# A transformer and two mixer layers in one kernel: the first modulated norm by quarters instead of halves, with the other modulation pieces loaded behind each round's weights

## The reference

```python
mod = silu(c) @ w_ada + b_ada                 # c: 1 x 1024, w_ada: 1024 x 6144
sh1, sc1, g1, sh2, sc2, g2 = split(mod, 6)
h = rms_norm(x, norm1_g) * (1 + sc1) + sh1    # 256 x 1024
proj = h @ w_in                               # 1024 x 12800: rq, rk, rv, rg, 9 attention tiles, 2 gates
...                                           # retention: rotary, scores, group norm per head, gate
x = x + g1 * token_mixer(h)
h = rms_norm(x, norm2_g) * (1 + sc2) + sh2    # and so on
```

## Time and profile before

| what | us |
| --- | --- |
| median of 3 runs (1368.62 to 1371.56) | 1368.72 |
| the profiled execution | 1369.16 |
| its span, first to last instruction | 1367.4 |
| TensorE busy | 1309.5 |
| VectorE busy | 881.9 |
| ScalarE busy | 736.4 |
| GpSimd busy | 638.9 |

### The profile page before, as it was taken

The page is one execution under the profiler, slowest core; times in us unless marked ns, Lnnn a source line. Parts: engine busy times, 40 slices in busy tenths (PEclk is TensorE's granted clock), DMA queues, the critical chain, the costliest instruction groups (busy, mean ns, idle before and its releaser), DMA issues.

```text
span 1367.4 us, 18658 instructions
## 1 busy us (share of the span) xinstructions
PE 1309.5 (96%) x6684; PEld 1085.4 (79%) x6684; DVE 881.9 (64%) x1383; ACT 736.4 (54%) x1107; POOL 638.9 (47%) x512
## 2 busy tenths in 40 slices
PE   7999999999998999999999999999989999899997
PEld 4778787899886788888787787888868877788885
DVE  6684873345343565223678667888868867788777
ACT  5343444444464544445566428666745663567664
POOL 3898888988858699999400420000051034000000
...
GB/s 375 312 262 305 157 243 292 242 182 245 187 154 142 167 185 188 197 191 183 203 127 81 1 21 315 313 289 336 281 186 182 94 31 1 222 316 293 283 312 97
DMA packets 45496, 280.03 MB, mean 205 GB/s; under 512 B 5565, under 2 KB 8893, under 8 KB 13918
## 3 DMA queue, kind: packets, MB, share of 16 engines
...
## 4 chain that ended last, share of the span: by engine, by line
PE 74%; DVE 11%; POOL 5%; DVEq 3%; ACT 3%; issue 2%; DMA 1%; ACTq 1%; SPq 0%; POOLq 0%
PE AC L1302 9%; PE AC L1304 9%; PE AC L1303 9%; PE G L1302 8%; PE G L1304 8%; PE G L1303 8%; POOL w_lo L721 5%; PE T L1492 2%; PE G L1492 2%; DVE w_lo L2172 2%; DMA w_raw<-w_stream 1%; PE G L1340 1%; PE G L1339 1%; PE G L1338 1%; PE T L1493 1%
## 5 line engine op out<-in xcount | busy, mean ns | idle before, releaser
L721 POOL TENSOR_TENSOR w_lo<-w_raw,w_hi 128x512 fp32r<-128x512 f32 (+1 forms) x470 | 610.5, 1334 | 332.5 <-ACT w_hi L784 321.0
L784 ACT ACTIVATE w_hi<-w_raw 128x1024 fp32r<-128x1024 f32 x444 | 467.0, 1058 | 392.1 <-PE AC L1304 172.4
L2172 DVE TENSOR_TENSOR w_lo<-w_raw,w_hi 128x1024 fp32r<-128x1024 f32 x228 | 275.7, 1224 | 52.6 <-ACT w_hi L784 44.7
L1302 PE MATMUL AC<-w_hi,yT_hi 128*128 128x512 f32 x368 | 145.3, 395 | 0.9 <-POOL w_lo L721 0.9
L1304 PE MATMUL AC<-w_hi,yT_lo 128*128 128x512 f32 x368 | 142.7, 388 | 0.0
L1303 PE MATMUL AC<-w_lo,yT_hi 128*128 128x512 f32 x368 | 142.5, 387 | 0.0
L1302 PE MATMUL G<-w_hi,arena_r 128*128 128x512 f32 x320 | 128.2, 401 | 4.3 <-DVE w_lo L3042 2.2
L1304 PE MATMUL G<-w_hi,arena_r 128*128 128x512 f32 x320 | 125.1, 391 | 0.0
L1303 PE MATMUL G<-w_lo,arena_r 128*128 128x512 f32 x320 | 124.7, 390 | 0.0
L1302 PE MATMUL G<-w_hi,xT 128*128 128x512 f32 (+1 forms) x240 | 98.5, 410 | 5.4 <-DVE xT L2324 2.1
L1302 PE MATMUL AC<-w_hi,xT 128*128 128x512 f32 x240 | 98.4, 410 | 3.4 <-POOL w_lo L721 3.4
...
## 6 DMA issues: line engine op xcount, KB each, us to landing
...
```

Source lines behind the costliest of these rows:

```text
L721: i = pool.tensor_tensor(w_lo[:, k % SLOTS, cols], w_raw[:, raw, cols], w_hi[:, k % SLOTS, cols].bitcast(F32), ALU.subtract)
L784: act.activation(w_hi[:, k % SLOTS, :], w_raw[:, raw, :], ACT.Copy).then_inc(hi_ready, 1)
L1302: pe.matmul(out, xh, wh, start=start, stop=False)
L2172: dve.tensor_tensor(w_lo[:, k % SLOTS, :], w_raw[:, k % RAW, :], w_hi[:, k % SLOTS, :].bitcast(F32), ALU.subtract).then_inc(lo_ready, 1)
```

## The change

The first norm goes by quarters of 256 channels. The scaled tokens (`x` times the inverse root, by ScalarE) are turned on TensorE before shift and scale, so that these are columns with one value per partition: a quarter's sums over partitions are four narrow matmuls (`quarter_sums`), and VectorE applies them to each chunk of 128 channels with one `tensor_scalar` (`turned_quarter`). `ada_quarter` sums 512-wide products, most of them in PSUM; the last product of quarter 0 is made by TensorE. The first three tiles are built quarter by quarter (unit order 3u + j). The bias rows are three matmul groups of four rows, stored once; ScalarE's queue issues a copy in DRAM that repeats them 128 times, at tile 5. The lows of units 10 and 11 are VectorE's. In the SP program, `ada_piece(r - 1)` is issued behind the three weight pieces of round r, where piece r was issued before; VectorE's program from `cst_loaded` to the second norm isn't changed. The host packs the same weights in another order, and shift, norm gain and `c` come as columns.

The diff, cut to its core (a row of dots stands for what is left out, and eight blanks of indent are taken off):

```diff
 ADA_ORDER = (1, 0, 2, 3, 4, 5)
 N_ADA = len(ADA_ORDER)
 U_MIX = 16 * 6
...
-ADA_PE = range(0, 3)
-ADA_FIRST = sum(len(r) for r in ADA_DVE)
-DVE_LO = [U_RET_IN, U_RET_IN + 2 * SLOTS] + [U_RET_IN + UP * j - 1 for j in (11, 12, 13)]
+QUARTERS = 4
+QC = KC // QUARTERS
+QW = 2 * QC * P
+ADA_FIRST = QUARTERS * KC
+N_SUMMED = QUARTERS - 2
+PE_SUM = KC - 1
+DVE_LO = [U_RET_IN + 10, U_RET_IN + 11] + [U_RET_IN + UP * j - 1 for j in (11, 12, 13)]
 U_JOINED = U_ATT_FIRST + UP
...
-    return U_RET_IN + 2 * PRE * (u // 2) + 2 * j + u % 2
+    return U_RET_IN + PRE * u + j
...
-def turn_bank(c, t):
-    return (AC[:, 2 + t, :], T[:, t, :])[c]
...
+    return T[:, q % 2, :]
+def sum_bank(q):
+    return T[:, (q + 1) % 2, :]
+def sum_cols(q):
...
-    def first_weights(s):
-        sp.wait_ge(ada_used, PIECE * (s + 1))
-        piece(2 * n_ring + s, s)
-    def second_half(q):
-        for s in range(PIECE):
-            sp.dma_start(half_home[PIECE * q + s], A["w_stream"][n_ring + q][:, s * UNIT:(s + 1) * UNIT]).then_inc(half_landed[q], 16)
-    sp.wait_ge(onehot_round, len(GROUPS))
-    second_half(0)
-    first_weights(0)
...
-    sp.wait_ge(bias_row, N_AH)
-    for q in range(1, KC // PIECE):
-        second_half(q)
-    first_weights(2)
-    for s in range(2):
-        lows_done(PIECE * (s + 1))
-        piece(3 * n_ring + s, s)
+    piece(0, 2)
+    piece(1, 3)
...
+    def first_units(s):
+        for u in range(PIECE):
+            sp.dma_start(w_raw[:, s * PIECE + u, :], A["w_stream"][2 * n_ring + s][:, u * UNIT:(u + 1) * UNIT]).then_inc(raw_landed[s], 16)
+    def quarter(q):
+        for h in range(2):
+            sp.dma_start(quarter_home[2 * q + h], A["w_stream"][2 * q + h]).then_inc(quarter_landed[2 * (q % 2) + h], 16)
+    first_units(0)
+    quarter(1)
+    first_units(1)
+    sp.wait_ge(ada_used, KC // 2)
+    piece(2 * n_ring + 2, 2)
+    quarter(2)
+    lows_done(PIECE)
+    piece(3 * n_ring, 0)
+    sp.wait_ge(ada_used, 2 * KC)
+    quarter(3)
+    lows_done(2 * PIECE)
+    piece(3 * n_ring + 1, 1)
     sp.dma_start(arena[:, 19968:20480], A["const1"][:, 1536:2048]).then_inc(cst_loaded, 16)
     sp.wait_ge(ada_used, KC)
     piece(3 * n_ring - 1, n_ring - 1)
...
-    for r in range(1, U_MIX // (RAW - PIECE)):
-        for s in range(2 if r == 1 else 0, n_ring):
-            if s == n_ring - 1:
-                sp.wait_ge(ada_used, ADA_FIRST + PIECE * r)
-            else:
-                lows_done((RAW - PIECE) * (r - 1) + PIECE * (s + 1))
+    def ada_piece(i):
+        sp.wait_ge(ada_used, ADA_FIRST + PIECE * i)
+        piece((i + 2) * n_ring + n_ring - 1, n_ring - 1)
+    rounds = U_MIX // (RAW - PIECE)
+    for r in range(1, rounds):
+        for s in range(2 if r == 1 else 0, n_ring - 1):
+            lows_done((RAW - PIECE) * (r - 1) + PIECE * (s + 1))
             piece((r + 2) * n_ring + s, s)
+        if r >= 2:
+            ada_piece(r - 1)
...
         if s == n_ring - 1:
+            ada_piece(rounds - 1)
             sp.wait_ge(ada_used, ADA_FIRST + (N_ADA - 2) * KC)
...
-        if k == 1:
-            pool.wait_ge(h_ready, TOK)
-        if k == 7:
-            pool.wait_ge(h_ready, HALVES * TOK)
...
-    for h in range(N_AH):
-        act.wait_ge(bias_row, h + 1)
-        act.activation(bias_vec[:, h, :], row_banks[h % len(row_banks)], ACT.Copy).then_inc(bias_rows_out, 1)
...
-    def half_rows(c, shift, scale):
-        act.wait_ge(scale_sum, c + 1)
-        act.activation(mod1[:, c, 1, :], scale, ACT.Copy).then_inc(scale_out, 1)
-        act.wait_ge(mod_sum, c + 1)
-        act.activation(mod1[:, c, 0, :], shift, ACT.Copy).then_inc(mod_out, 1)
...
-    turned_half(0)
-    his(U_RET_IN + 1, U_RET_IN + 2 * SLOTS)
-    half_rows(1, T[:, 0, :], T[:, 1, :])
-    act.wait_ge(bias_rows_out, N_AH)
-    act.dma_start(A["rel_scratch"][:, 0:P, :].rearrange("h p n -> p h n"), bias_vec).then_inc(bias_stored, 16)
...
+    act.wait_ge(rstd_done, 1)
+    for t in range(TOK):
+        act.activation(xs[:, t, :], x_sb[:, t, :], ACT.Copy, scale=var[t]).then_inc(h_ready, HALVES)
...
+    def turned_quarter(q):
+        for i in range(QC):
+            act.wait_ge(h_turned, QC * q + i + 1)
+            act.activation(xT_hi[:, QC * q + i, :], h_full[:, i * S:(i + 1) * S], ACT.Copy).then_inc(chunk_hi, 1)
+    his(U_RET_IN, U_RET_IN + 2)
+    turned_quarter(0)
+    for g in range(len(GROUPS)):
+        act.wait_ge(bias_row, g + 1)
+        act.activation(bias_vec[:, g, :], row_banks[g], ACT.Copy).then_inc(bias_rows_out, 1)
+    his(U_RET_IN + 2, U_RET_IN + PRE + 2)
+    for q in range(1, QUARTERS):
+        turned_quarter(q)
+        his(U_RET_IN + PRE * q + 2, U_RET_IN + min(PRE * (q + 1) + 2, PRE * UP - 1))
+    act.wait_ge(bias_rows_out, len(GROUPS))
+    act.dma_start(A["rel_scratch"][:, P, :].rearrange("(g h) n -> h g n", h=AH), bias_vec).then_inc(bias_stored, 16)
...
-            act.wait_ge(h_ready, HALVES * TOK)
+            act.wait_ge(bias_stored, 16)
+            act.dma_start(A["rel_scratch"][:, 0:P, :], A["rel_scratch"][:, P:P + 1, :].to_broadcast([N_AH, P, NT])).then_inc(bias_stored, 16)
+            act.wait_ge(chunk_lo, KC)
             act.dma_start(mod[:, 0:2048], A["gn_g"].partition_broadcast(P)).then_inc(gn_loaded, 16)
             act.dma_start(W, A["gn_b"].partition_broadcast(P)).then_inc(gn_loaded, 16)
...
+    def bias_rows_of(g):
+        pe.wait_ge(onehot_round, g + 1)
...
-    def half_chunk(s, shift, scale):
-        pe.wait_ge(half_landed[s // PIECE], 16 * PIECE)
-        for v, out in ((1, scale), (0, shift)):
-            pe.matmul(out, csil[:, s:s + 1].to_broadcast([P, P]), half_home[s][:, v * NT:(v + 1) * NT], start=s == ADA_PE[0], stop=False)
...
-    def half_sums(c, shift, scale):
-        pe.wait_ge(ada_summed, c + 1)
-        for v, out, done_sem in ((1, scale, scale_sum), (0, shift, mod_sum)):
-            pe.matmul(out, ones_col.to_broadcast([P, P]), mod1[:, c, v, :], start=c == 0, stop=True).then_inc(done_sem, 1)
...
-    for h in range(N_AH):
-        bias_row_of(h)
...
-    half_sums(0, AC[:, 2, :], AC[:, 3, :])
-    half_chunk(0, T[:, 0, :], T[:, 1, :])
+    def quarter_turn(q):
+        for i in range(QC):
+            for t in range(TOK):
+                c = QC * q + i
+                pe.transpose(turn_bank(q)[:, i * S + t * P:i * S + (t + 1) * P], xs[:, t, c * P:(c + 1) * P], ident[:, :])
+    def quarter_sums(q):
+        pe.wait_ge(ada_summed, q + 1)
+        for i in range(2 * QC):
+            o = pe.matmul(sum_cols(q)[:, i:i + 1], mod1[:, q, i * P:(i + 1) * P], ones_col, start=True, stop=True)
+        o.then_inc(scale_sum, 1)
...
+    pe.wait_ge(c_ready, 1)
+    pe.wait_ge(raw_landed[3], 16)
+    for i in range(2 * QC):
+        at = (PE_SUM - KC // 2) * QW + i * P
+        o = pe.matmul(G[:, 1, i:i + 1], quarter_home[1][:, at:at + P], csil[:, PE_SUM:PE_SUM + 1], start=True, stop=True)
+    o.then_inc(scale_sum, 1)
+    pe.wait_ge(h_ready, HALVES * TOK)
+    quarter_turn(0)
+    quarter_sums(0)
+    keep_busy(G[:, 0, :], 8)
...
-    for c in range(HALVES):
-        for t in range(TOK):
...
+    for u in range(QUARTERS):
         for j in range(PRE):
-            for u in (2 * c, 2 * c + 1):
-                k = first_unit(j, u)
-                if (c, j, u) == (0, 0, 1):
-                    for s in (1, 2):
-                        half_chunk(s, T[:, 0, :], T[:, 1, :])
-                if (c, j, u) == (0, PRE - 1, 1):
-                    half_sums(1, T[:, 0, :], T[:, 1, :])
...
-                i.then_inc(unit_used, 1)
+            k = first_unit(j, u)
+            if u == 0 and j == 1:
+                pe.wait_ge(bias_rows_out, len(GROUPS))
+            if j == PRE - 1 and u + 1 < QUARTERS:
+                quarter_sums(u + 1)
...
+            for t in range(TOK):
+                for q in range(QC):
+                    ch, w = QC * u + q, slice(q * NT, (q + 1) * NT)
+                    if (j, t) == (0, 0):
+                        pe.wait_ge(chunk_lo, ch + 1)
+                    i = mm3(pre_banks[j][:, t, :], xT_hi[:, ch, t * P:(t + 1) * P], xT_lo[:, ch, t * P:(t + 1) * P],
+                            w_hi[:, k % SLOTS, w], w_lo[:, k % SLOTS, w], ch == 0, ch == KC - 1)
+            i.then_inc(unit_used, 1)
+            if j == 0 and u + 1 < QUARTERS:
+                quarter_turn(u + 1)
...
-    def ada_half(c):
-        m = mod[:, c * D:(c + 1) * D]
-        for s in ADA_DVE[c]:
-            if c == 0:
-                dve.wait_ge(raw_landed[s // PIECE], 16)
+    def ada_quarter(q, s0, s1):
+        last = KC - 1 if q else PE_SUM - 1
+        for s in range(s0, s1):
+            h = s // (KC // 2)
+            if s % (KC // 2) == 0:
+                dve.wait_ge(quarter_landed[2 * (q % 2) + h] if q else raw_landed[2 + h], 32 if q == 3 else 16)
+            w = quarter_home[2 * q + h][:, s % (KC // 2) * QW:(s % (KC // 2) + 1) * QW]
+            if s == 0:
+                dve.tensor_scalar(mod1[:, q, :], w, csil[:, 0:1], None, ALU.mult).then_inc(ada_used, 1)
```

(93 more changed lines are left out.)

96 lines of the change are left out of this document (39 added, 57 removed).

## The result

| | median us (lowest to highest) |
| --- | --- |
| before | 1368.72 (1366.54 to 1371.56, 5 runs) |
| after | 1411.24 (1409.57 to 1411.51, 5 runs) |

The changed kernel is slower: ratio 1.0301, 95% interval 1.0288 to 1.0315, or +42.5 us where 19.3 were forecast (1388). The profiled execution took 1411.51 us, with a span of 1409.7.

What follows compares the result with a forecast made beforehand. TensorE was taken as the bound, busy for 96% of the span with 74% of the chain. Front -3.5, pieces 4 to 6 +15, down projection +8 gave +19.5 us: 1388 us as a median, range 1373 to 1398.

Steps and rivals of the forecast that it cites:

- The front by itself: First norm by quarters: unit 12 starts near 69 us instead of 72.46, leaving a gain of 3.5 us (0 to 8).
- the turn: Down projection, at 232.95 us in the old trace: it waits 4 to 5 us for lows delayed by late piece 9.
- unit 66: Down projection, six units after piece 9's stall: late piece 10 meets the same pattern, costing 3.5 to 4 us.
- Rival (a): Late pieces are covered by VectorE's idle time before group norm 0; only the front counts: 1365 us, chance 0.12.
- rival (b): Only the down projection pays, as the group norm stage packs tighter: about 1373 us, chance 0.15.
- rival (c): The front has no lead or loses, and the stalls reach their upper bounds: 1392 to 1398 us, chance 0.11.
- After 260 us nothing changes: Sign expected in the trace: no further change in the kernel after 260 us.
- that only fills slots while TensorE waits for rotate(1): Before unit 12: weight pieces issued earlier, as SP no longer waits for piece 0, only fill slots.
- The bias table's copy in DRAM ... is hidden: ScalarE's DMA queue: the 3 MB copy is hidden, first read by the attention; group norm rows used after 135 us.
- The term of 15: Late pieces 4 to 6 hold up group norms and roots, so unit 45 starts 15 us late (bounds 6 and 19).
- that of 8: Down projection: late pieces 9 and 10 stall two turns, 8 us in sum (bounds 6 and 10).
- 7.4 us: Landing time assumed for each late modulation piece, counted from the end of the lows it follows.

Runs made afterwards that it cites:

- e1: The changed kernel with SP's order of the modulation pieces as before the change: 1365.9 us, ratio 0.9982.
- e3: The changed kernel with the old order of the modulation pieces and the copy in DRAM issued behind the norm rows: 1366.7 us.
- e5: The changed kernel with the copy behind the norm rows and only modulation pieces 1 to 7 one round late: 1393.0 us.
- e11: The changed kernel with the copy behind the norm rows and only modulation pieces 1 to 3 one round late: 1372.4 us.
- e2: The changed kernel with the copy in DRAM issued behind the norm rows, all pieces still one round late: 1405.8 us.
- e6: The changed kernel with the copy behind the norm rows and only modulation pieces 8 to 15 one round late: 1379.5 us.
- e4: The kernel before, with only the modulation pieces issued one round later and no copy in DRAM: 1415.2 us, ratio 1.0335.
- e7: The changed kernel with the copy behind the norm rows and every modulation piece late by a third of a round: 1365.6 us.
- e8: The changed kernel with the copy behind the norm rows and every modulation piece late by two thirds of a round: 1374.3 us.

## Why the prediction was wrong

**The direction and the places were right, the sum was short by 23 us.** Unit 0 at 21.37 was forecast for 20 to 21; the idle time before unit 12 ended with rotate(1)'s reads at 71.4, forecast 69. The front by itself is worth 3.1 us (e1), forecast 3.5, but that is luck in part: in e1 and e3 the hole before unit 12 ends with GpSimd's lows and not with rotate(1), and in the changed kernel, where rotate(1) does end it, the lead at unit 12 is 1.1 us and not 3.5. TensorE's holes at unit 37 (8.73 us, forecast 7), unit 43 (4.62, forecast 6), the turn (4.98, forecast 4 to 5) and unit 66 (3.99, forecast 3.5 to 4) stand where the chain of steps put them. Rival (a) falls with the result, rival (b) with e5, and rival (c), a front without lead, with e1. "After 260 us nothing changes" was too early: the second stall of the down projection stands at 290.

**The steps that failed.**

1. Pieces 1 to 3 had no term, and they cost 5.8 us (e11). I took the late pieces from piece 4 on, because there a root waits behind them. But rotate(3) stands behind piece 2 in VectorE's program (14.02 us of waiting), and a turn before unit 20 needs it. And of the earlier weights the prediction said "that only fills slots while TensorE waits for rotate(1)": they also set GpSimd to work beside pieces 0 and 1 and so made rotate(1) itself later, and unit 12 with it by 3.3 us (e11 against e3). Piece 1's products alone, 4.32 us in the changed kernel and 2.66 before, are 1.7 of the 2.4 us between 71.4 and the forecast 69.
2. "The bias table's copy in DRAM ... is hidden". I looked at who reads the data, and not at what ScalarE's queue does behind the copy. Its next issue took 8.40 us, and hi(28) to hi(30) waited for it (the expectation for e2 misnumbers them). The lows that release piece 4, lo(29), were finished at 130.2 us instead of 125.9 in e2, and the piece landed 12.47 us after its issue instead of 10.38, so that its products start 6.4 us later. Alone the queue's order is free (e1 against e3); with the late pieces it costs 5.5 us (after against e2).
3. The term of 15 for pieces 4 to 6 measured 20.6 (e5 less e11, with piece 7 in it), that of 8 for pieces 9 and 10 12.8 (e6). From unit 36 to unit 45, the stretch of the 15, the changed kernel lost 17.7 us (27.96 late less 10.24). The turns of the chain I had nearly right: from piece 4 to 5 and on to 6 they take 26.5 and 30.3 us in e2 (136.72, 163.18, 193.50), forecast 25.1 and 29.1. What was short is its start, piece 4. Its lows ended at 125.9 in e2 instead of 123.4 before, although the front begins 7 us sooner, and the landing took longer. I took 7.4 us from one pair, of which 0.4 is the issue before its own; from its own issue to its landing piece 4 took 8.13 us in e4, where there is no copy in DRAM, 10.38 in e2 and 12.47 in the changed kernel. (Its last step is also added up wrongly: 193.5 and 7.5 are 201.0, not 200.6.) In the down projection the waits were right, 8.97 us against 8. What I left out there is the unit behind each hole, at 1.2 GHz: 4.56 us for unit 60 (267.26 to 271.82) and 4.45 for unit 66, where 2.75 is normal, 3.5 us for the two. With the waits that is 12.5 of the 12.8.

The prediction sets 6.8 us from the Trainium skill (DMA: Bandwidth & Descriptors, section Anatomy of one DMA) beside its 7.4; the page fits that to DMAs that GpSimd issues, and SP issues these. Four later pieces took 6.84 to 7.33 us, so the figure was near, but neither it nor the 7.4 holds for piece 4.

The sum as measured: -2.3 (e3) + 5.8 + 20.6 + 12.8 + 5.5 = +42.4, against +42.5 for the change. What the prediction never asked is how much delay is free: by e7 and e8 a third of it costs nothing, and the last third costs most.

How the 17.7 us between unit 36 and unit 48 divide can be read from the traces. e2 needs 57.24 us from the start of one to the start of the other (160.01 to 217.25) and e3 39.55. The waits shown are 13.6 us longer in e2, and units 37 and 43, behind holes, take 4.24 and 4.97 us instead of 2.72 each, 3.8 more, at a granted clock of 0.64 and 0.54 instead of 1.00. That is 17.4 of the 17.7. Not settled: what a full clock alone would give back there, since TensorE might only wait longer for the loop. And the kernel time that the copy's packets cost, beside its place in the queue, was not tried apart; the landings of piece 4 show only that it comes later with the copy under way.
